# Output projections in plain 32-bit products, and the second expert's weights loaded meanwhile

## What is computed

```python
y = jnp.concatenate([h_loc, h_mem], axis=-1) @ w_out[i]      # (512, 1024) @ (1024, 1024)
x = layer_norm(ALPHA * x + y, ln1_g[i], ln1_b[i])
m = grouped_moe(x, router_w, router_b, w_gate[i], w_up[i], w_down[i])
x = layer_norm(ALPHA * x + m, ln2_g[i], ln2_b[i])
```

## Time and profile before

| | |
|---|---|
| three runs | 1694.94, 1695.75, 1700.8 us |
| median | 1695.75 us |
| span of the profiled execution (its own time is not listed) | 1693.4 us |
| TensorE busy (matmuls) | 1334.5 us, 79% |
| VectorE busy | 458.4 us, 27% |
| ScalarE busy | 261.7 us, 15% |
| mean granted TensorE clock | 0.890 |
| moved by DMA | 495.76 MB, 293 GB/s over the span |

### The profile page before, as it was taken

The page is one execution under the profiler, slowest core; times in us unless marked ns, Lnnn a source line. Parts: engine busy times, 40 slices in busy tenths (PEclk is TensorE's granted clock), DMA queues, the critical chain, the costliest instruction groups (busy, mean ns, idle before and its releaser), DMA issues. The chain is left out here.

```text
span 1693.4 us, 15769 instructions
## 1 busy us (share of the span) xinstructions
PE 1334.5 (79%) x5966; PEld 708.7 (42%) x5966; DVE 458.4 (27%) x886; ACT 261.7 (15%) x459; POOL 111.5 (7%) x121
## 2 busy tenths in 40 slices
PE   6999885987887877881699995868888878878870
PEld 5887672322232222331477774653322222222230
DVE  2335664110100001005633238572101000000006
ACT  2222320000000000003343213410000000000002
POOL 0000011000000000002100000101000000000003
PEclk9999996998998899896799997878989989999995
DMA  9511437999999999995122020467999999999964
GB/s 281 170 48 28 181 142 314 397 421 421 421 421 421 421 421 420 422 400 206 50 100 73 26 100 1 199 247 289 419 422 421 422 421 421 421 421 422 421 284 174
DMA packets 109221, 495.76 MB, mean 293 GB/s; under 512 B 11640, under 2 KB 32120, under 8 KB 60024
## 3 DMA queue, kind: packets, MB, share of 16 engines
q1 hardware_dynamic: 91512, 453.21, 66.1%
q0 software_dynamic: 7424, 25.17, 4.0%
q10 hardware_dynamic: 10240, 16.79, 2.7%
HBM read 472.07 MB, written 23.07 MB: 292 GB/s over the span
## 5 line engine op out<-in xcount | busy, mean ns | idle before, releaser
L920 PE MATMUL bank<-ring,xT 128*64 128x512 f32 x2048 | 515.1, 661 | 158.1 <-DMA ring<-in_w_up 156.3
L920 PEld LDWEIGHTS bank<-ring,xT 128*64 128x64 f32 x2048 | 166.3, 152 | 464.6 <-issue 463.1
L944 PE MATMUL bank<-ring,hidT 128*64 128x512 f32 x1024 | 237.2, 606 | 3.4 <-issue 3.4
L1015 DVE COPY xT<-bank 128x512 f32<-128x512 f32 x64 | 44.3, 692 | 689.0 <-PE bank L906 689.0
L980 ACT ACTIVATE xT<-bank 128x256 f32<-128x256 f32 x64 | 24.6, 384 | 682.2 <-PE bank L920 682.2
L944 PEld LDWEIGHTS bank<-ring,hidT 128*64 128x64 f32 x1024 | 70.1, 138 | 122.3 <-issue 115.3
L895 POOL DMA_INDIRECT xT<-x_rows,block_rows x64 | 60.8, 950 | 877.7 <-PE bank L906 803.4
L986 ACT COPY y<-bank 128x512 f32<-128x512 f32 x64 | 37.5, 586 | 250.4 <-PE bank L944 250.4
L1025 DVE COPY hidT<-bank 128x256 f32<-128x256 f32 x64 | 27.2, 425 | 174.5 <-PE bank L930 174.5
L477 PE MATMUL bank<-x_half_hi,w_half_hi 128*128 128x512 f32 x160 | 63.6, 397 | 1.4 <-issue 1.4
L272 POOL TENSOR_TENSOR x_sb<-x_sb,ln_b 128x1024 f32<-128x1024 f32 x12 | 28.3, 2360 | 541.7 <-DVE x_sb L260 541.7
(11 more groups left out here) (244 smaller groups left out, 1360.5 us busy)
## 6 DMA issues: line engine op xcount, KB each, us to landing
ring<-in_w_gate SPq DMA_DIRECT2D x62, 2048.0 KB, 28.6
ring<-in_w_up SPq DMA_DIRECT2D x62, 2048.0 KB, 33.2
ring<-in_w_down SPq DMA_DIRECT2D x62, 2048.0 KB, 24.3
expert_rows<-y ACTq DMA_DIRECT2D x128, 128.0 KB, 6.7
ring<-in_mlstm_w_in SPq DMA_DIRECT2D x6, 2048.0 KB, 7.8
ring<-in_conv_w_in SPq DMA_DIRECT2D x18, 512.0 KB, 6.1
ring<-in_w_out SPq DMA_DIRECT2D x2, 4096.0 KB, 14.9
ring<-in_w_kv_mem SPq DMA_DIRECT2D x2, 2048.0 KB, 11.2
```

Of the source, the lines that this page charges most:

```text
L920: last = nc.tensor.matmul(GU_BANK[j][64 * f:64 * f + 64, :], xgT[j][:, c, 64 * h:64 * h + 64], gu[:, :, h, c, 256 * f:256 * f + 256], star ...
L944: last = nc.tensor.matmul(Y_BANK[j][64 * n:64 * n + 64, :], hidT[j][:, c, 64 * f:64 * f + 64], dn[:, f, c, 512 * n:512 * n + 512], start=( ...
L1015: nc.vector.tensor_copy(xgT[j].rearrange("p c r -> p (c r)"), X_BANK[:, :]).then_inc(xcopied, 1)
```

## The change

In both layers the output projections multiply `headsT` and `w_out_sb` as they are, as plain 32-bit operands, one call per piece and slice in place of three. The rounding by ACT, the subtraction by DVE and their two counters are gone; TensorE waits once for the output weights. As R1 is free in this stage now, expert 1 is loaded into it right behind expert 0. When the eight pieces are done, gate and up of expert 2 follow into R2, and its down weights behind the store of the last normed tile; the load at the head of the expert stage is gone. `load_gate_up` issues two loads of 2048 KB and `load_down` one.

```diff
@@ -619,27 +619,23 @@
                           ("C", 1), ("P", 1), ("C", 2), ("C", 3)]
                 POS_BANK, CODE_BANK = (bank[7], bank[0]), bank[1]
 
-                hi_ready, lo_ready = s("p1_hi"), s("p1_lo")
-                w_half = halves_at(f"w_out_half_{l}", [P, KT, D_MODEL], ring_at + 4 * W_EXP, ring_at + 4 * 2 * W_EXP)
-                h_half = halves_at(f"heads_half_{l}", [P, KT, SEQ], ring_at + 4 * (W_EXP + 8192),
-                                   ring_at + 4 * (2 * W_EXP + 8192))
                 with nc.Block() as block:
                     @block.sync
                     def _(sp):
                         for row, dst in ((ln1_g, ln_g), (ln1_b, ln_b)):
                             sp.dma_start(dst[:, :], row[l].unsqueeze(0).broadcast_to([P, D_MODEL])).then_inc(in_ln, 16)
 
-                        load_gate_up(sp, l, 0, 0, in_gu[l][0])
-                        load_down(sp, l, 0, 0, in_dn[l][0])
+                        for e in range(2):
+                            load_gate_up(sp, l, e, e, in_gu[l][e])
+                            load_down(sp, l, e, e, in_dn[l][e])
                         for t in range(TT):
                             if t == TT - 1:
                                 sp.wait_ge(out_done, 2 * TT)
-                                load_gate_up(sp, l, 1, 1, in_gu[l][1])
+                                load_gate_up(sp, l, 2, 2, in_gu[l][2])
                             sp.wait_ge(normed, t + 1)
                             sp.dma_start(x1_dram[l].rearrange("(t p h) d -> p t (h d)", t=TT, h=2)[:, t, :],
                                          x_sb[:, t, :]).then_inc(stored, 16)
-                        load_down(sp, l, 1, 1, in_dn[l][1])
-                        load_gate_up(sp, l, 2, 2, in_gu[l][2])
+                        load_down(sp, l, 2, 2, in_dn[l][2])
                         sp.wait_ge(stored, 16 * TT)
 
                     @block.gpsimd
@@ -649,21 +645,19 @@
                     @block.tensor
                     def _(pe):
                         def project(t, n, k):
-                            w, h = (a[:, k, n * 512:(n + 1) * 512] for a in w_half), (a[:, k, t * P:(t + 1) * P] for a in h_half)
-                            (w_hi, w_lo), (h_hi, h_lo) = w, h
-                            for i, (a, b) in enumerate(((h_hi, w_hi), (h_lo, w_hi), (h_hi, w_lo))):
-                                last = nc.tensor.matmul(bank[2 * (t % 2) + n][:, :], a, b, start=(k == 0 and i == 0),
-                                                        stop=(k == KT - 1 and i == 2))
+                            last = nc.tensor.matmul(bank[2 * (t % 2) + n][:, :], headsT[:, k, t * P:(t + 1) * P],
+                                                    w_out_sb[:, k, n * 512:(n + 1) * 512], start=(k == 0),
+                                                    stop=(k == KT - 1))
                             if k == KT - 1:
                                 last.then_inc(out_done, 1)
 
+                        pe.wait_ge(in_w_out[l], 16)
                         for kind, t in script:
                             if kind == "O":
                                 if t >= 4:
                                     pe.wait_ge(summed, t - 3)
                                 for k in range(KT):
                                     if t == 0:
-                                        pe.wait_ge(lo_ready, k + 1)
                                         project(0, 0, k)
                                         project(0, 1, k)
                                     else:
@@ -723,11 +717,6 @@
 
                     @block.scalar
                     def _(act):
-                        act.wait_ge(in_w_out[l], 16)
-                        for k in range(KT):
-                            nc.scalar.copy(w_half[0][:, k, :], w_out_sb[:, k, :])
-                            nc.scalar.copy(h_half[0][:, k, :], headsT[:, k, :]).then_inc(hi_ready, 1)
-
                         for kind, t in [("L", 0), ("L", 1), ("T", 0), ("R", 0), ("L", 2), ("T", 1), ("R", 1), ("T", 2),
                                         ("R", 2), ("L", 3), ("T", 3), ("R", 3)]:
                             if kind == "L":
@@ -813,12 +802,6 @@
                                                 ALU.is_equal).then_inc(marked, 1)
 
 
-                        dve.wait_ge(in_w_out[l], 16)
-                        for k in range(KT):
-                            dve.wait_ge(hi_ready, k + 1)
-                            V.tensor_tensor(w_half[1][:, k, :], w_out_sb[:, k, :], w_half[0][:, k, :], ALU.subtract)
-                            V.tensor_tensor(h_half[1][:, k, :], headsT[:, k, :], h_half[0][:, k, :],
-                                            ALU.subtract).then_inc(lo_ready, 1)
                         dve.wait_ge(in_ln, 32)
                         for t in range(3):
                             residual_and_norm(t)
@@ -868,8 +851,6 @@
                             load_gate_up(sp, l, e, r, in_gu[l][r])
                             sp.wait_ge(y_done, e - 2)
                             load_down(sp, l, e, r, in_dn[l][r])
-                        sp.wait_ge(gathered[0], 16)
-                        load_down(sp, l, 2, 2, in_dn[l][2])
                         with sp.Fori(0, 9) as i:
                             for r in range(3):
                                 load(3 * i + (3 + r), r)
```

## The result

| | before | changed |
|---|---|---|
| runs | 1694.94, 1695.75, 1695.8, 1700.8 us | 1707.24, 1708.14, 1710.46, 1712.46 us |
| median | 1695.78 us | 1709.3 us |
| ratio, 95% interval | | 1.008, 1.0064 to 1.0096 |
| span of the profiled execution (its own time) | 1693.4 us | 1708.8 us (1710.46 us) |

The kernel became slower by 13.5 us (10.9 to 16.3 by the interval). The forecast was 1708.3 us, with 1700 to 1716 as its range.

A forecast was written before the change was run, and what follows sets the result against it. Weight loads were taken to bound the expert stages, a chain through the other engines the stages between. T2's delays, 5.1 us in layer 0 and 7.4 in layer 1, added 12.5 to 1695.75: 1708.3 us, range 1700 to 1716.

The forecast's parts named there:

- The price of a plain call: TensorE, output projections: a call is two instructions of 0.429 us, 0.858 us; 64 calls take 54.9 us a layer.
- The bounds: Limits on a plain instruction's price in the projections: 0.419 us from line 920, 0.446 us from line 199.
- The start: Projection stage: first product 0.2 us behind the stage's start without the halves, a gain of 3.4 us per layer.
- T and R: TensorE, projection stage between T0 and T2: two T and two R cost 5.47 us beside the products.
- The clock: TensorE at the projections' start: full speed in layer 0, half at first in layer 1, costing 2.2 us there.
- The sum to T2: From the projection stage's start to T2: 60.6 us in layer 0, 62.8 in layer 1; 5.1 and 7.4 later.
- What is late next: End of the projection stage: DVE waits for ACT's square root, which hangs on T2, so T2's delay passes on whole.
- The moved loads: Moving down of expert 2 ahead of the expert stage is worth nothing; 5.9 idle us of queue time hide it.
- One sign named for it: Layer 0's expert stage: loads keep their distances from the first gather on, 10.9 us to the load of expert 3.
- Cheap plain products: Rival, projections: a call costs 0.443 us, so the kernel gets 40.5 us faster, 1655 us; chance 0.05.
- Bare weight loads: Rival, projections: each of 128 weight loads a layer adds 0.190 us, 24.3 us per layer more, 1757 us; chance 0.04.
- Paying loads: Rival, expert stage: weights streaming ahead give back 5.0 us per layer, 1698.3 us; chance 0.10.

The follow-up runs named there:

- experiments 7 to 10: Changed kernel, and kernel of experiment 4, with four extra unread products before layer 1's projections (1710.68, 1690.56 us), then with seven (1707.42, 1689.94 us).
- experiment 3: Changed kernel, with TensorE's first product in the projections also waiting for the layer norm's rows: 1723.44 us, ratio 1.0168.
- experiment 1: Changed kernel's plain products with the load order of the kernel before: 1710.23 us, ratio 1.009.
- experiment 2: Kernel before, with only the load of down of expert 2 moved to the end of the projection stage: 1700.71 us, ratio 1.0038.
- experiment 5: Changed kernel with four of the eight slices in every projection, so sums are partial: 1663.05 us, ratio 0.9799.
- experiment 4: Kernel before, with pieces O0 and O1 alone as plain products on raw operands, the rest three products: 1691.54 us, ratio 0.9966.
- experiments 7 and 8: Changed kernel (7) and kernel of experiment 4 (8), with four extra unread products in layer 1's last mixer wait: 1710.68 and 1690.56 us.
- experiments 9 and 10: As experiments 7 and 8, with three more extra products right behind layer 1's last mixer transposes: 1707.42 and 1689.94 us.

## Why the prediction was right

- **The price of a plain call.** Predicted 0.858 us from line 472 lengthened by 213 ns; measured 0.861. Adding the longer stream to the spacing of the shorter one was the right way: from 256 to 512 columns the distance grew by 0.2145 us, as much as the stream (0.213), and the weight load stayed hidden. The bounds (0.838 and 0.892) weren't needed.
- **The start.** Predicted 0.2 us behind the stage's first load; measured 0.04. The gain there was 3.5 us and not 3.4.
- **T and R.** 5.47 us for two of each; in the changed kernel 32.79 - 64 x 0.4305 = 5.24 us between T0 and T2.
- **The clock.** Full in layer 0 and halved at first in layer 1, both as predicted; the cost of 2.2 us there was 2.4, and experiments 7 to 10 show that it is the clock. The rise came 5 us into the products, where the prediction had reckoned with 3 to 6; its 2.2 was a value picked inside that range, not derived.
- **The sum to T2.** 60.6 and 62.8 predicted, 60.38 and 62.78 measured. In layer 0 the start was 0.16 shorter, the calls 0.2 longer (64 of 0.861 make 55.1) and T and R 0.23 shorter, so the errors cancelled in part.
- **What is late next.** DVE waits for ACT, and ACT for T2, as predicted; experiment 3 and the constant 30.5 us from T2 to the first gather show that delays pass whole.
- **The moved loads.** Predicted at nothing, and the pair of experiment 1 and the changed kernel bears it out within some 4 us. One sign named for it did not come: from the first gathered rows to the load of expert 3 are 12.07 us in layer 0 (292.77 - 280.70) and not 10.9; the clock was full later in that execution, and the time was made up later. What the prediction didn't see is how narrow this is. In the kernel before, the loads behind T2 end 2 us ahead of the first gather, and the down load can only stand ahead of the barrier because expert 1 was moved out of its way; alone it costs 0.4% (experiment 2). The prediction named the queue time behind the barrier as the cover and left out the gather as the one that a load ahead of it would delay.
- **The rivals.** Cheap plain products fell by the row of line 648 and by experiment 5. Bare weight loads fell by the same row: 190 ns of load stand inside a spacing of 430. That contradicts the rule of the Trainium skill (TensorE: Matmul & The Clock Gate, section "Part 3: Packing small matmuls — row/col tiling") that a load overlaps products in flight only when the row groups differ. The same section of the Trainium skill also lets a load into the background weight buffer go ahead of products in flight. The prediction left that out, and the row doesn't contradict it. Paying loads fell by experiment 1.
- **What is left.** 1.2 us between the stages' delays and the medians; with one profile of each kernel they can't be told from what differs between executions.

## What to carry to other kernels

Count what a cheaper-looking form costs on the engine that sets the stage: one plain call in place of three products looks like less work, but is 0.86 us against 0.68, and only the wait for the halves paid for a part of it. Where preparing operands keeps the bound engine waiting, use the form that needs no preparation for the first pieces alone, as in experiment 4, and the cheaper one for the rest. Before moving a load forward, look for what it will stand ahead of, also across a barrier: a prefetch that is still under way at the next stage's first gather (0.4% here) costs more than one that is issued later into an idle queue (nothing that could be seen).

## What the runs showed of the hardware

- A plain 32-bit product of 128 columns of weights and 512 streamed is two instructions, 0.4305 us apart at full clock, while a product in the rounded type takes 0.2267 us; weight loads of 190 and 188 ns lie inside these spacings.
- TensorE's clock can be full at the start of a dense stretch and fall about 1 us into it, after 2.65 us of idle time (experiments 7 and 8); with 0.95 us and more products ahead of it (experiments 9 and 10), or with 1.57 us (layer 0 of the changed kernel) it stayed.
- From the issue of the first gather to the transposes that wait for it are 3.2 to 3.8 us where the weight loads have ended before, and 5.1 and 5.9 us in experiment 2, where they still run.
